# A 24th weight slot for the expert stage, paid for with single buffers, in a decoder layer on one core

## What is computed

```python
t = h2.reshape(-1, D)                      # 256 tokens x 1024
g_logits = t @ w_rg + b_rg                 # 4 groups
g_sel = argmax(g_logits); p_grp = softmax(g_logits)[g_sel]
e_logits = (t @ w_re + b_re).reshape(T, 4, 8)[g_sel]
topv, topi = top_k(softmax(e_logits), 2)   # 2 experts in the chosen group
gate = onehot(g_sel) * w_e * p_grp
for gi in range(4):                        # 4 groups x 8 experts = 32 experts
    a = einsum('td,edf->tef', t, w_e1[gi])
    b = einsum('td,edf->tef', t, w_e3[gi])
    y += einsum('tef,efd->td', silu(a) * b * gate[:, gi, :, None], w_e2[gi])
x = x + gt2 * y
return rmsnorm(x, norm_f)
```

## Time and profile before

| what | us |
|---|---|
| median of 3 runs (433.51 to 435.42) | 433.85 |
| the profiled execution's own time | 434.87 |
| its span, first to last instruction | 433.0 |
| PE busy | 378.6 (87%) |
| DVE, ACT, POOL busy | 187.9, 171.5, 156.0 |
| DMA packets' time, share of 16 engines | 92.0% |
| moved | 163.23 MB, mean 377 GB/s |

### The profile page before, as it was taken

One profiled execution on the slowest core, in us unless ns is written; L12 is line 12 of the kernel. 1 busy time (PEld: TensorE's weight loads), 2 busy tenths in 40 slices (PEclk: granted clock), 3 DMA queues, 4 the chain that ended last, 5 costly groups with the idle time before them and its releaser, 6 DMA issues.

```text
span 433.0 us, 8010 instructions
## 1 busy us (share of the span) xinstructions
PE 378.6 (87%) x3348; PEld 297.0 (69%) x3348; DVE 187.9 (43%) x402; ACT 171.5 (40%) x325; POOL 156.0 (36%) x125
## 2 busy tenths in 40 slices
PE   6899999999999999999989898989894694783983
PEld 6689999899899999999967463636361351450440
DVE  3998366889787477463252212030303003001014
ACT  3667757797359466243443311112020030030023
POOL 0799898869773767986000000000000000000000
PEclk9999999999999999999989999999999599699798
DMA  8999999666999997999892999999999999999972
GB/s 332 421 420 421 418 420 408 273 251 232 426 419 420 421 379 257 428 381 351 326 427 102 422 422 422 420 424 415 421 419 420 422 422 423 419 419 419 419 320 98
DMA packets 23223, 163.23 MB, mean 377 GB/s; under 512 B 2576, under 2 KB 2704, under 8 KB 4368
## 3 DMA queue, kind: packets, MB, share of 16 engines
q1 hardware_dynamic: 23184, 162.68, 92.0%
HBM read 161.62 MB, written 1.05 MB: 376 GB/s over the span
## 4 chain that ended last, share of the span: by engine, by line
PE 73%; DMA 15%; DVE 5%; SPq 4%; ACT 1%; issue 1%; DVEq 0%
PE bank L1448 29%; PE bank L1823 11%; DMA ring<-in_e 7%; DMA late<-in_e 6%; PE bank L1492 5%; PE bank L1779 5%; PE cs_b L1834 5%; PE bank L1768 4%; SPq L451 4%; PE bank L1497 2%; DMA ring<-in_mod 2%; PE cs_b L1448 1%; PE bank L1700 1%; DVE ring L882 1%; PE bank L1729 1%
## 5 line engine op out<-in xcount | busy, mean ns | idle before, releaser
L527 POOL TENSOR_TENSOR ring_r<-ring,his_r 128x512 fp32r<-128x512 f32 x120 | 155.7, 1335 | 36.1 <-ACT his_r L550 35.9
L803 ACT ACTIVATE raw<-bank,sm 128x128 f32<-128x128 f32 x60 | 22.5, 456 | 118.7 <-PE bank L1779 118.7
L550 ACT ACTIVATE his_r<-ring 128x2048 fp32r<-128x2048 f32 (+1 forms) x32 | 57.6, 1801 | 19.0 <-DMA ring<-in_rest 12.3
L1823 PE MATMUL bank<-ring,raw 128*32 128x256 f32 x480 | 54.1, 414 | 7.9 <-DMA his<-in_e 7.9
L1297 DVE TENSOR_TENSOR tmp<-bank,tmp 128x256 f32<-128x256 f32 x7 | 3.0, 425 | 121.0 <-ACT tmp L812 121.0
L1448 PE MATMUL bank<-his_r 128*128 128x256 f32 x288 | 41.4, 286 | 0.0
L1823 PEld LDWEIGHTS bank<-ring,raw 128*32 128x32 f32 x480 | 26.5, 119 | 20.5 <-issue 11.6
L1823 PE MATMUL bank<-his,raw 128*32 128x256 f32 x240 | 33.8, 427 | 7.4 <-DMA ring<-in_e 7.1
L1448 PEld LDWEIGHTS bank<-his_r 128*128 128x128 f32 x288 | 36.9, 191 | 1.8 <-issue 1.8
L935 DVE CUSTOM_DVE_ANT_0 ring<-ring,cs_b 128x1024 f32<-128x1024 f32 x32 | 37.7, 1216 | 0.2
L1779 PEld LDWEIGHTS bank<-o_att,gm 128*128 128x128 f32 x240 | 30.0, 201 | 6.6 <-issue 6.6
(11 more groups left out here) (350 smaller groups left out, 725.4 us busy)
## 6 DMA issues: line engine op xcount, KB each, us to landing
ring<-in_rest SPq DMA_DIRECT2D x40, 1024.0 KB, 11.1
ring<-in_e SPq DMA_DIRECT2D x40, 1024.0 KB, 23.7
his<-in_e SPq DMA_DIRECT2D x16, 1024.0 KB, 24.4
home<-in_e SPq DMA_DIRECT2D x10, 1024.0 KB, 26.3
ring<-in_block SPq DMA_DIRECT2D x8, 768.0 KB, 20.7
free_unit<-in_e SPq DMA_DIRECT2D x5, 1024.0 KB, 26.0
o_att<-in_e SPq DMA_DIRECT2D x5, 1024.0 KB, 26.0
const<-in_e SPq DMA_DIRECT2D x4, 1024.0 KB, 19.2
```

The costliest lines, as they stand in the source:

```text
L527: pool.tensor_tensor(ring_r[:, slot_of(n), sl], ring[:, slot_of(n), sl], hi(d)[:, sl].bitcast(F32), ALU.subtract).then_inc(s["w_lo"], 1)
L550: act.activation(hi(d)[:, 0:WIDTH[d]], ring[:, slot_of(n), 0:WIDTH[d]], ACT.Copy).then_inc(s["w_hi"], 1)
L803: ins = act.activation(xg[:, b, k, :], source[:, j * P:(j + 1) * P], ACT.Identity, bias=S("B2", KD)[:, k:k + 1], scale=S("A2", KD)[:, k:k ...
L1823: ins = pe.matmul(up_bank[e * CAP:(e + 1) * CAP, half], xg[:, b, k, e * CAP:(e + 1) * CAP], wt[e][:, k, :], start=(k == 0), stop=(k == KD ...
```

## The change

- The router's scratch moves from `v` into the second half of `tmp`; `xg` becomes a single buffer in `v`; sigmoid, product and hidden values share one tile; the gated outputs go to the second half of `tmp` and to the part of the constants that is read no more (`SPENT`). That leaves `raw` free: it becomes the slot `RAW`, released at "brm3", and `XSLOTS` is 24.
- With a single `xg`, `gather(1)` moves behind `up("w3")` on PE, and the sigmoid ahead of the two `gather_half` on ACT.
- The router's group logits are padded to 8 columns by the weights and biases, so `lg` has 40 columns for each token block (before 36), and DVE's MEMSET and COPY of `g8` (L1207, L1213) go.
- PE gets `keep_busy` with 7 products of 128x256 ahead of its wait for `mask_r`.
- The first four reloads (the slots of the first quad's w1) are issued in two pieces of 0.5 MB: the first halves after k = 3 of `up("w1")` (new semaphore `half_w1`), the second halves after `used`.

```diff
-XSLOTS = SLOTS + 9
+XSLOTS = SLOTS + 10
...
-            (LAST[1], "sum16"), (LAST[2], "bra1"), (LAST[3], "bra3"), (LAST[4], "brm1"), (MQK, "brm3"), (LAST[5], "brm3")]
+            (LAST[1], "sum16"), (LAST[2], "bra1"), (LAST[3], "bra3"), (LAST[4], "brm1"), (MQK, "brm3"), (RAW, "brm3"), (LAST[5], "brm3")]
...
+SPENT = CONSTS["tri"][0]
+assert NCONST - SPENT >= 512
...
-        router = v[:].rearrange("p t n -> p (t n)")
+        router = tmp[:, 1, :]
...
-        sig, act_a, hid = tmp[:, 0, 0:F], tmp[:, 0, F:2 * F], tmp[:, 1, 0:F]
-        hidT = flat[:, 3 * F:3 * F + 2 * P].rearrange("p (f n) -> p f n", f=2)
+        sig = act_a = hid = tmp[:, 0, 0:F]
+        hidT = tmp[:, 0, F:F + 2 * P].rearrange("p (f n) -> p f n", f=2)
...
-        xg = raw[:, :, 0:256].rearrange("p k (b n) -> p b k n", b=2)
-        outs = v
+        xg = v[:].rearrange("p t (k n) -> p (t k) n", k=KD // 2)
+        outs = (const[:, SPENT:SPENT + 512], tmp[:, 1, :])
...
+        def pieces(n):
+
+            return 2 if 0 <= n - NPRE - XSLOTS < QUAD else 1
+
...
-            for m in range(XSLOTS, NU):
+            for part, gone in ((0, s["half_w1"]), (1, used)):
+                for e in range(QUAD):
+                    m = XSLOTS + e
+                    w, i = QUAD_UNITS[m % QU]
+                    sl = slice(part * (UNIT // 2), (part + 1) * (UNIT // 2))
+                    sp.wait_ge(gone, e + 1)
+                    sp.dma_start(slot(slot_of(NPRE + m))[:, sl], w_e[w][m // QU * QUAD + i][:, sl]).then_inc(
+                        landed[slot_of(NPRE + m)], 16)
+            for m in range(XSLOTS + QUAD, NU):
                 sp.wait_ge(used, m - XSLOTS + 1)
                 load(slot_of(NPRE + m), m // QU, m % QU)
...
             def quad(it, b, last=False):
+                act.wait_ge(used, it * QU + UP_UNITS)
+                act.activation(sig, up_bank[:, 0:F], ACT.Sigmoid).then_inc(s["sig_r"], 1)
                 if not last:
                     gather_half(1 - b, 0, it * 2 + 3)
                     gather_half(1 - b, 1, it * 2 + 4)
-                act.wait_ge(used, it * QU + UP_UNITS)
-                act.activation(sig, up_bank[:, 0:F], ACT.Sigmoid).then_inc(s["sig_r"], 1)
...
-            lg, g8 = R("lg", TT, 36), R("g8", TT, 8)
-            link(dve.memset(g8, -3.0e38))
+            lg = R("lg", TT, NR)
+            g8 = lg[:, :, 0:8]
...
-            link(dve.tensor_copy(g8[:, :, 0:G], lg[:, :, 0:G]))
...
             ps = take("rank")
+            keep_busy(ps[:, 0:T], both_consts, 7)
             pe.wait_ge(s["mask_r"], 1)
...
+                        if k == KD // 2 - 1 and isinstance(r, int) and r + j == 0 and w == "w1":
+                            ins.then_inc(s["half_w1"], 1)
                         if k == KD - 1:
                             ins.then_inc(used, 1)
...
                 scatter(1 - b, False).then_inc(s["scat"], 1)
+                up("w3", r, j, b)
                 if not last:
                     pe.wait_ge(s["g_evac"], it * 2 + 3)
                     gather(1)
-                up("w3", r, j, b)
-                if not last:
                     pe.wait_ge(s["g_evac"], it * 2 + 4)
```

More of the change, by code:

```diff
@@ L30 @@
 NE = G * E
+NR = 8 + NE
 QUAD = 4
@@ L113, in hi_slot @@
     return RING + [UNIT_JOB[n] for n in DENSE].index(job) % HI
-HT, QKT, GM, MQK, LATE, X_HOME, XN_HOME, ATT, SPARE, BIASES = range(SLOTS, SLOTS + 10)
+HT, QKT, GM, MQK, LATE, X_HOME, XN_HOME, ATT, SPARE, BIASES, RAW = range(SLOTS, SLOTS + 11)
 MOD_HOME = (RING - 2, RING - 1, GM, MQK, X_HOME, XN_HOME, ATT, QKT)
@@ L154 @@
 for _name, _shape in (("cols", (NROWS,)), ("ident", (P,)), ("ones", (P,)), ("w_if", (KD, 8)), ("b_if", (1,)),
-                      ("stack", (8,)), ("alibi", (HEADS, 384)), ("mask", (384,)), ("lam", (4, DA_HD)), ("tri", (P,)),
-                      ("b_r", (G + NE,)), ("w_r", (KD, G + NE)), ("slot", (TT, QUAD, CAP)), ("iota8", (TT, 8))):
+                      ("alibi", (HEADS, 384)), ("mask", (384,)), ("lam", (4, DA_HD)), ("slot", (TT, QUAD, CAP)), ("tri", (P,)),
+                      ("b_r", (NR,)), ("w_r", (KD, NR)), ("iota8", (TT, 8)), ("stack", (8,))):
     CONSTS[_name] = (NCONST, _shape)
@@ L177, in constants @@
     put("lam", np.stack([np.asarray(inputs[f"lam_{n}"])[0] for n in ("q1", "k1", "q2", "k2")])[None])
-    put("b_r", np.concatenate([np.asarray(inputs["b_rg"])[0], np.asarray(inputs["b_re"])[0]])[None])
-    w_r = np.concatenate([np.asarray(inputs["w_rg"])[0], np.asarray(inputs["w_re"])[0]], axis=1)
-    put("w_r", w_r.reshape(KD, P, G + NE).transpose(1, 0, 2))
+    put("b_r", np.concatenate([np.asarray(inputs["b_rg"])[0], np.full(8 - G, -3.0e38), np.asarray(inputs["b_re"])[0]])[None])
+    w_r = np.concatenate([np.asarray(inputs["w_rg"])[0], np.zeros((D, 8 - G)), np.asarray(inputs["w_re"])[0]], axis=1)
+    put("w_r", w_r.reshape(KD, P, NR).transpose(1, 0, 2))
     put("ones", np.ones((P, P)))
@@ L301, in K @@
             return ap
+        both_consts = const[:, CONSTS["ident"][0]:CONSTS["ident"][0] + 2 * P]
         ident, ones, cols, w_r, b_r, lamv = K("ident"), K("ones"), K("cols"), K("w_r"), K("b_r"), K("lam")
@@ L367, in build @@
             sem(n) for n in ("x_in", "xT_in", "const_in", "const2_in", "nf_in", "out_done"))
-        landed = [sem(f"landed{i}") for i in range(SLOTS + 10)]
+        landed = [sem(f"landed{i}") for i in range(SLOTS + 11)]
         used = sem("used")
@@ L384, in slot_of @@
             return place(n) if n < NPRE else ORDER[(n - NPRE) % XSLOTS]
+        def pieces(n):
+            return 2 if 0 <= n - NPRE - XSLOTS < QUAD else 1
         def landed_value(n):
-            return 16 * sum(slot_of(m) == slot_of(n) for m in range(n + 1))
+            return 16 * sum(pieces(m) for m in range(n + 1) if slot_of(m) == slot_of(n))
         def landed_total(i):
-            return 16 * sum(slot_of(m) == i for m in range(NPRE + NU))
+            return 16 * sum(pieces(m) for m in range(NPRE + NU) if slot_of(m) == i)
         def slot(i):
@@ L789, in _ @@
             for tt in range(TT):
-                act.activation(R("gexp", TT, G)[:, tt, :], R("lg", TT, 36)[:, tt, 0:G], ACT.Exp,
+                act.activation(R("gexp", TT, G)[:, tt, :], R("lg", TT, NR)[:, tt, 0:G], ACT.Exp,
                                bias=R("ngmax", TT)[:, tt:tt + 1],
@@ L802, in gather_half @@
                     k = 4 * half + j
-                    ins = act.activation(xg[:, b, k, :], source[:, j * P:(j + 1) * P], ACT.Identity,
+                    ins = act.activation(xg[:, k, :], source[:, j * P:(j + 1) * P], ACT.Identity,
                                          bias=S("B2", KD)[:, k:k + 1], scale=S("A2", KD)[:, k:k + 1])
@@ L1069, in _ @@
             dve.wait_ge(*full("rb"))
-            release(dve.tensor_tensor(rbias[:], pb("rb")[:, 0:G + NE], b_r[:], ALU.add), "rb")
+            release(dve.tensor_tensor(rbias[:], pb("rb")[:, 0:NR], b_r[:], ALU.add), "rb")
             dve.wait_ge(*free("rb"))
@@ L1822, in up @@
                     for e in range(QUAD):
-                        ins = pe.matmul(up_bank[e * CAP:(e + 1) * CAP, half], xg[:, b, k, e * CAP:(e + 1) * CAP],
+                        ins = pe.matmul(up_bank[e * CAP:(e + 1) * CAP, half], xg[:, k, e * CAP:(e + 1) * CAP],
                                         wt[e][:, k, :], start=(k == 0), stop=(k == KD - 1), tile_position=(0, e * CAP))
+                        if k == KD // 2 - 1 and isinstance(r, int) and r + j == 0 and w == "w1":
+                            ins.then_inc(s["half_w1"], 1)
                         if k == KD - 1:
```

29 lines of the change are left out of this document (14 added, 15 removed).

## The result

| | before | changed |
|---|---|---|
| median of 20 runs each, us | 434.09 | 436.9 |
| lowest and highest | 433.22, 436.08 | 433.25, 439.6 |
| ratio, 95% interval | | 1.0066 (1.0043 to 1.0089) |
| profiled execution, its span | 434.87, 433.0 | 433.37, 431.5 |

The change makes the kernel slower by 0.66%, and it spreads the runs: from under 3 us to over 6. The forecast was 429.4 us, in a range of 428.0 to 432.4. The profiled execution is one of the three fastest of the 20; what it shows of PE is therefore the mild case. The mean granted clock of each run is on record: 0.957 in the three fastest (433.25 to 433.37 us), 0.942 to 0.946 in the seven slowest (439.1 to 439.6).

What follows compares the result with a forecast made beforehand. Transfers were taken as the bound, through the last w3's landing: -2.50 - 1.73 - 0.6 = -4.8, giving 430.0 from the profiled 434.87 or 429.0 from the median 433.85. Forecast 429.4 us, range 428.0 to 432.4.

Steps and rivals of the forecast that it cites:

- What bounds the kernel: Expert stage to the end: transfers never pause after one hole; compute's last 22.1 us follow the landing of the last w3.
- The 24th slot: Before the hole in the loads: one more 1.049 MB unit loaded early, 72 left instead of 73, -2.50 us.
- The two pieces: Restart after the hole: first reloads wait for k = 3 of the first w1, not k = 7, -1.73 us.
- Rival three: First reloads: the halves are slow, each additional transfer paying a start; 3 to 6 us lost, 432.4 to 435.4, chance 0.05.
- The mask: PE's mask wait before the first gather: filler overshoots by 0.95, full clock gives back 1.54, together -0.6 us.
- The single buffers: PE's quads: chain 2.3 us longer, 23.1 a quad, costing 0 while a quad stays under the transfers' 25.0 us.
- The slack of 11.7 us: PE before the last quad: it could start at 387.3, may start as late as 399.0; 1.9 us a quad.
- rival one: Quads: single buffers make PE the bound, half clock after gaps, over 25.0 us a quad; 436 to 437, chance 0.07.

## Why the prediction was wrong

**What bounds the kernel.** Right for the kernel before, and for the changed one once PE is helped: the earlier trace rows come back, with the last w3 landing at 407.97 (branch moved) instead of 410.86. For the changed kernel as it stands it is wrong: there PE sets the end.

**The 24th slot, -2.50.** Right: 2.3 us between 23 and 24 slots where the transfers are the bound (433.5 and 431.18), and 1.1 MB. In the changed kernel itself nothing of it can be seen (436.37 with 23 slots, 436.9 with 24), since it is not the transfers that set its end.

**The two pieces, -1.73.** Wrong. The reload went out earlier, as worked out, but the halves moved at 355 GB/s instead of 405 and gave the time back (431.18 with, 431.24 without). I took the rate from the 0.75 MB blocks. Rival three had the direction but not the size: with a start for each additional transfer it came to 3 to 6 us, and the pieces cost about 1.7 us in all, as much as their early start had been worked out to gain. The Trainium skill, "DMA: Bandwidth & Descriptors", section "Bandwidth", advises transfers of 1 MiB or more; the trace agrees in the direction, with 355 GB/s beside 405. In the kernel as changed, where PE sets the end, whole reloads were not faster but slower, by 1.7 us (438.58).

**The mask, -0.6.** The first gather takes 1.82 us at a clock of 1.00, as said, and the filler overshoots. On the median it is nothing: 434.7 beside 434.09. The sum took the fall of the clock there as the likely case; in the profile of the kernel before with the halves alone it doesn't come, after the same wait.

So the transfers came forward by 2.9 us in place of 4.8 (410.86 to 407.97): 2.3 to 2.5 for the slot, the small rest for all that stands before the restart.

**The single buffers, 0.** This is the step that failed. The length of the chain was right: 23.1 worked out, 22.93 measured in the quad that kept its clock. The slack of 11.7 us was right in its arithmetic too. Two things ate it. First, the step held the quad at full clock and put the fall into rival one, with 0.07. Rival one named the mechanism and the point, 25.0 us a quad; the profile has quads of 24.6 to 26.7, and one of 22.9. What spoke for a low chance were the old quads, whose gaps were shorter than the new ones; that is no evidence for the new ones. The price of rival one, 436 to 437 us, holds the measured 436.9 partly by luck: it stood for 3.1 us of loss in each quad and nothing for the branch, and the profile has 2.2 a quad and 3.5 for the branch, in a run of 433.37. Second, the 3.5 us of the branch between quads 6 and 7 were not in the sum at all. They must have lain hidden in the 7.12 us of the earlier trace rows. A wait of an engine tells when it stopped waiting, not what else it did meanwhile; I used the slack up to the landing as if PE could reach it without the branch. 13.0 + 3.5 - 11.7 = 4.8, as much as the gain that had been forecast: in the profiled run the last w3 starts at 410.40, not at 406.0, and hardly ahead of the 411.00 of the earlier trace rows. Its weights had landed some 2.6 us before: SP issues that load at 381.44, in the run with the branch moved at 381.64, where it lands at 407.97, so here at about 407.8 (an estimate). (Its span is 1.5 us shorter all the same: 0.6 here, the rest in the tail, where most of it lies behind the issue of the output's stores.) The median run is 3.5 us longer still. No profile shows such a run. Its clock is lower (0.950 to 0.954 in the runs from 436.4 to 436.6), but how its 3.5 us divide between the quads and the stall at the branch isn't shown.

That the falls are a cause is shown by the fillers, and that the stall is the branch's by taking it out and by moving it: either one alone brings the median to 432.44 or 431.83, both together to 431.18, where the transfers set the end. With either one gone, the change is faster than the kernel before.

## What to carry to other kernels

Here the slack of an engine was used up by three things that no busy row of the old kernel showed: a longer chain, half clock in new gaps, and what had been hidden in the old wait (the load of a flag and a branch). Before buffers are given up for slots, put the longer chain on the chip with fillers in its gaps; with them, and with the branch moved to where PE waits anyway, the same 24 slots are 0.6% faster than the kernel before instead of 0.7% slower. That PE had become the bound, with a clock that differs from run to run, showed first in the spread of the runs: 6.4 us in the changed kernel, 0.8 in the version with fillers and the branch moved.

## What was not expected of the hardware

With four loads of 1 MB cut in two by columns, the 8 us behind the restart moved 317 to 385 GB/s, where whole ones moved 387 to 405, with the DMA engines as busy; cut by partitions 221. A flag's load and a branch on PE took 3.5 to 4.6 us, and in four profiles another 0.43 to 1.55 us came some 40 products later. Two idle gaps of 1.9 and 1.6 us, with some 2 us of products between them, preceded half clock in five of six quads. With 4 and 3 filler products of 0.43 us in those gaps the clock stayed at 1.00 in quads 1 to 5. One idle gap of 1.9 us ahead of the first gather was followed by a clock of 0.51 in one profile and of 1.00 in another.
